# Half of the second expert table read in one pass through a token-by-expert weight matrix, with all gathers of the first table ahead of those of the second

## The reference

```python
best, pos = lax.top_k(cand, PEER_TOPK)                        # 8 heads x 16 experts per token
expert_idx = jnp.take_along_axis(cand_idx, pos, axis=-1)
gates = jax.nn.softmax(best, axis=-1).astype(h.dtype)
...
act = jnp.einsum('td,thkd->thk', xb, u_tab[ib])
w = gb * jax.nn.gelu(act, approximate=False)
return jnp.einsum('thk,thkd->td', w, v_tab[ib])
```

## Time and profile before

| what | value |
|---|---|
| time, median of 3 runs | 2583.87 us (2572.18 to 2584.49) |
| profiled execution: span from first to last instruction | 2569.2 us |
| around the span, median of the runs less the span | 14.7 us |
| PE / DVE / POOL / ScalarE busy | 76% / 50% / 32% / 10% |
| bytes moved by DMA | 793 MB, of which 606 MB by POOL's queue |

### The profile page before, as it was taken

The page is one execution under the profiler, slowest core; times in us unless marked ns, Lnnn a source line. Parts: engine busy times, 40 slices in busy tenths (PEclk is TensorE's granted clock), DMA queues, the critical chain, the costliest instruction groups (busy, mean ns, idle before and its releaser), DMA issues.

```text
span 2569.2 us, 20124 instructions
## 1 busy us (share of the span) xinstructions
PE 1958.5 (76%) x7000; PEld 1310.4 (51%) x7000; DVE 1286.4 (50%) x1645; ACT 266.1 (10%) x521; POOL 824.4 (32%) x583
## 2 busy tenths in 40 slices
PE   0399999998999999896895569557855774586557
PEld 0388888887888888785332223223322332232223
DVE  8634587773222221488644754474456324532553
ACT  0012122111000000201111001100101010001001
POOL 1000000000000000033555655565566555655652
PEclk9999999999999999998997789778877987897788
DMA  9867765662434354177999999999999999999996
GB/s 399 371 248 305 292 284 221 250 261 109 153 136 158 134 222 151 56 302 327 361 392 392 392 391 393 389 374 387 392 383 369 402 390 367 366 411 389 400 362 269
DMA packets 92366, 793.07 MB, mean 309 GB/s; under 512 B 10657, under 2 KB 10657, under 8 KB 11313
## 3 DMA queue, kind: packets, MB, share of 16 engines
q0 software_dynamic: 78512, 606.14, 59.0%
q1 hardware_dynamic: 13824, 186.55, 18.8%
q10 hardware_dynamic: 2, 0.02, 0.0%
HBM read 790.57 MB, written 2.10 MB: 309 GB/s over the span
## 4 chain that ended last, share of the span: by engine, by line
PE 57%; DMA 16%; issue 9%; DVE 8%; POOL 8%; ACT 1%; POOLq 0%; DVEq 0%; SPq 0%; ACTq 0%
PE ps L559 26%; PE ps L720 19%; DMA arena<-expert_u,u_now 11%; PE ps L567 9%; POOL arena L370 7%; DMA arena<-ada 3%; DVE arena L1018 3%; DMA arena<-expert_v,v_now 2%; DVE mod_rows L761 1%; DVE work L857 1%; DVE work L854 1%; DVE buf_b L769 1%; PE ps L575 1%; PE ps L674 0%; POOL v_now L363 0%
## 5 line engine op out<-in xcount | busy, mean ns | idle before, releaser
L720 PE MATMUL ps<-arena,work 128*128 128x512 f32 x1520 | 698.1, 619 | 446.6 <-ACT work L534 284.8
L1018 DVE CUSTOM_DVE_ANT_0 arena<-arena,buf_b 128x2048 f32<-128x2048 f32 x256 | 586.0, 2293 | 427.6 <-DMA arena<-expert_u,u_now 424.4
L720 PEld LDWEIGHTS ps<-arena,work 128*128 128x128 f32 x1520 | 301.4, 200 | 837.5 <-issue 461.0
L370 POOL DMA_INDIRECT arena<-expert_u,u_now x256 | 477.7, 1866 | 293.1 <-DVE work L1018 142.3
L559 PE MATMUL ps<-buf_a,arena 128*128 128x256 f32 x2304 | 508.1, 382 | 10.9 <-DVE arena L875 5.2
L559 PEld LDWEIGHTS ps<-buf_a,arena 128*128 128x128 f32 x2304 | 440.9, 192 | 75.0 <-issue 14.7
L370 POOL DMA_INDIRECT arena<-expert_v,v_now x192 | 231.3, 1204 | 258.9 <-PE ps L720 216.7
L559 PE MATMUL ps<-arena 128*128 128x256 f32 x1024 | 223.7, 379 | 1.0 <-ACT arena L496 1.0
L720 PE MATMUL ps<-mod_rows,work 128*128 128x512 f32 x504 | 221.5, 592 | 0.0
L559 PEld LDWEIGHTS ps<-arena 128*128 128x128 f32 x1024 | 193.9, 190 | 27.3 <-issue 1.3
L350 POOL DMA_DIRECT2D arena<-ada x32 | 16.9, 529 | 529.4 <-DVE mod_rows L761 489.3
(11 more groups left out here) (194 smaller groups left out, 1010.1 us busy)
## 6 DMA issues: line engine op xcount, KB each, us to landing
arena<-weights SPq DMA_DIRECT2D x68, 2048.0 KB, 9.2
arena<-ada POOLq DMA_DIRECT2D x32, 2048.0 KB, 12.0
arena<-ada SPq DMA_DIRECT2D x16, 2048.0 KB, 16.3
arena<-expert_u,u_now POOLq DMA_INDIRECT x256
arena<-expert_v,v_now POOLq DMA_INDIRECT x192, 10.8
buf_a<-x_t SPq DMA_DIRECT2D x1, 2048.0 KB, 20.7
arena<-ln_rows POOLq DMA_DIRECT2D x1, 2048.0 KB, 7.4
buf_a<-x_rows SPq DMA_DIRECT2D x1, 2048.0 KB, 8.2
```

What stands on the lines that cost most here:

```text
L370: pool.indirect_dma_start(slots[s], None, table, bass.IndirectOffsetOnAxis(ap=indices[:, e:e + 1], axis=0)).then_inc(ring_loaded[s], 16)
L720: last = mm(ps[:, 4 * b + n, :], diag[:, s], v_slot[s][:, n * 512:(n + 1) * 512], start=first and e == 0, stop=False, skip_group_check=True)
L1018: v.tensor_tensor_reduce(out=u_slot[s], in0=u_slot[s], in1=h2[:, b], scale=1.0, scalar=0.0, op0=ALU.mult, op1=ALU.add, accum_out=sums[:, e ...
```

## The change

- Table `v` is split on the host by columns. Columns 0 to 1023 become `v_pass`, with the rows reordered so that 128 consecutive rows are the experts that share the second of the two key numbers (expert = 128 x first + second). Columns 1024 to 2047 become `v_side`.
- `v_side` is gathered as before, but with 4 KB per token, 0.524 MB per gather, in 5 slots, alternating between the blocks. DVE adds each gathered row, times its weight, into PSUM banks 4 to 7 (`add_row`).
- `v_pass` is read whole, once: 128 loads of 128 x 1024 (0.524 MB) by SP into 4 slots. PE multiplies each with a weight matrix [128 experts, 128 tokens] for each block, 4 products of 512 columns per load, into banks 0 to 3.
- The weight matrix is made in 64 groups of 4 tokens. For one token, the 128 slots are on the partitions: `first_hot` [slot, first key] is 1 where the slot's expert has that first key, `second_hot` [slot, second key] is the weight where it has that second key, and one PE product of the two gives the token's weights for all 16,384 experts, as 128 x 128. ScalarE copies a group from PSUM into `weight_t` (`keep_group`). The expert numbers and weights are transposed by PE for this.
- Groups 0 to 31 (block 0) are made beside the `u` gathers of block 1's heads 1 to 7, with `first_hot` built by ScalarE. Groups 32 to 63 (block 1) come after the last `u` row, with both built by DVE, and after each one `add_row`.
- All 256 gathers of `u` come first, in one ring of 8 slots, straight from `expert` without copies, and then the 256 of `v_side`. Loops over heads are written out.
- SP's first four pass loads wait only for the last choice (`s_gt`). PE starts the pass once all 64 groups are kept.
- On ScalarE the exponential of late choice n (`soft_exp`) stands between the gelus of heads n - 1 and n; the diagonals (L534), the three vector rows and `merge_block0`'s place in the middle go. Both blocks are merged and normalised at the end.
- `arena` grows to 8 chunks, `buf_b` moves into it, and the constants grow by 112 columns.

```diff
-U_RING, V_RING = 4, 8
-VECTOR_ROWS = (9, 11, 13)
+U_RING = 8
+SIDE = D_MODEL // 2
+PASS_RING, GATHER_RING = 4, 5
+GROUP = 4
+GROUPS = TOKENS // GROUP
+GROUP_BANKS = 3
...
+        u_first = [arena[:, n * row:(n + 1) * row] for n in range(4)] + [shift2, scale2]
+        u_slot = [u_first + [arena[:, n * row:(n + 1) * row] for n in pair] for pair in ((14, 15), (6, 7))]
+        weight_t = [arena[:, n * 4 * CHUNK:(n + 1) * 4 * CHUNK].rearrange("p (n t) -> p n t", t=P) for n in (1, 0)]
+        rows_out = chunk(5).rearrange("p (b n) -> p b n", b=BLOCKS)
+        gather_slot = [gate1[:, 0:SIDE], shift2[:, 0:SIDE], shift2[:, SIDE:], scale2[:, 0:SIDE], scale2[:, SIDE:]]
+        keys = cst[:, C_IOTA:C_END]
+        first_hot = cst[:, C_LEVELS:C_IOTA].rearrange("p (s t n) -> p s t n", s=2, t=GROUP)
+        second_hot = gate1[:, SIDE:].rearrange("p (s t n) -> p s t n", s=2, t=GROUP)
+        tail_slots = work[:, 0:PASS_RING * SIDE]
+        pass_slot = [tail_slots[:, n * SIDE:(n + 1) * SIDE] for n in range(PASS_RING)]
+        def groups_beside(n):
+            first = (n - HEADS - 1) * 5
+            return range(first, min(first + 5, GROUPS // BLOCKS))
...
+            sp.wait_ge(s_gt, BLOCKS * HEADS)
+            for n in range(N_KEYS):
+                s = n % PASS_RING
+                if n >= PASS_RING:
+                    sp.wait_ge(pass_used[s], n // PASS_RING)
+                sp.dma_start(pass_slot[s], v_pass[n * P:(n + 1) * P, :]).then_inc(pass_loaded[s], 16)
+                if n == 32 + PASS_RING:
+                    sp.dma_start(ln_slot[1], ln_rows[2:4, :].partition_broadcast(P)).then_inc(s_ln[1], 16)
...
+            def gather(table, into, b, e, loaded_sem):
+                pool.indirect_dma_start(into, None, table, bass.IndirectOffsetOnAxis(ap=expert[:, b, e:e + 1], axis=0))\
+                    .then_inc(loaded_sem, 16)
+            for n in range(BLOCKS * HEADS):
+                wait_alone(pool, s_ex, n + 1)
+                for e in range(TOPK):
+                    r = n * TOPK + e
+                    s, turn = r % U_RING, r // U_RING
+                    if turn:
+                        wait_alone(pool, u_used[s], turn)
+                    if r == SLOTS:
+                        for q in range(2):
+                            wait_alone(pool, used[q], 1 + F_END[q])
+                    gather(expert_u, u_slot[n // HEADS][s], n // HEADS, n % HEADS * TOPK + e, u_loaded[s])
+            for r in range(BLOCKS * SLOTS):
+                s, turn = r % GATHER_RING, r // GATHER_RING
+                if turn:
+                    wait_alone(pool, gather_used[s], turn)
+                elif s:
+                    wait_alone(pool, u_used[4 + (s - 1) // 2], BLOCKS * SLOTS // U_RING)
+                gather(v_side, gather_slot[s], r % BLOCKS, r // BLOCKS, gather_loaded[s])
...
+            def gelu(n):
+                act_e.wait_ge(u_used[U_RING - 1], (n + 1) * TOPK // U_RING)
+                run(gel[n % 2], act[n % 2], ACT.Gelu).then_inc(s_gel, 1)
+            def keep_weights_t(b):
+                act_e.wait_ge(s_wtp, b + 1)
+                run(wgt_t[:, b * P:(b + 1) * P], ps[:, 3, P:2 * P], ACT.Copy).then_inc(s_wt, 1)
+            def build_first_hot(g):
+                if g >= 2:
+                    act_e.wait_ge(s_grp, g - 1)
+                slot = first_hot[:, g % 2]
+                for t in range(GROUP):
+                    me.step(run(slot[:, t], keys, ACT.Abs, bias=first_t[:, g * GROUP + t:g * GROUP + t + 1], scale=-1.0))
+                me.settle()
+                run(slot, slot, ACT.Relu, bias=1.0, scale=-1.0).then_inc(s_fh, 1)
+            def keep_group(g):
+                act_e.wait_ge(s_grp, g + 1)
+                b, t = g // (GROUPS // BLOCKS), g % (GROUPS // BLOCKS) * GROUP
+                run(weight_t[b][:, :, t:t + GROUP], ps[:, g % GROUP_BANKS, :].rearrange("p (t n) -> p n t", t=GROUP), ACT.Copy)\
+                    .then_inc(s_grpe, 1)
+            gelu(0)
+            soft_exp(HEADS + 1)
+            for n in range(1, HEADS):
+                soft_exp(HEADS + 1 + n)
+                gelu(n)
+            keep_weights_t(0)
+            gelu(HEADS)
+            act_e.wait_ge(s_idx, 1)
+            for n in range(HEADS + 1, BLOCKS * HEADS):
+                for g in groups_beside(n):
+                    build_first_hot(g)
+                    if g:
+                        keep_group(g - 1)
+                gelu(n)
+            keep_group(GROUPS // BLOCKS - 1)
+            keep_weights_t(1)
+            for g in range(GROUPS // BLOCKS, GROUPS):
+                keep_group(g)
+            for b in range(BLOCKS):
+                rstd_of_ln(b, BLOCKS + 1 + b)
...
+            def transpose_experts(b):
+                pe.wait_ge(s_exr, b + 1)
+                nc.tensor.transpose(ps[:, 3, 0:P], expert_rows, ident).then_inc(s_ext, 1)
+            def transpose_weights(b):
+                pe.wait_ge(s_wgt, (b + 1) * HEADS)
+                pe.wait_ge(s_idx, BLOCKS)
+                nc.tensor.transpose(ps[:, 3, P:2 * P], gates[:, b], ident).then_inc(s_wtp, 1)
+            def multiply_groups(groups):
+                for g in groups:
+                    pe.wait_ge(s_fh, g + 1)
+                    pe.wait_ge(s_sh, g + 1)
+                    if g >= GROUP_BANKS:
+                        pe.wait_ge(s_grpe, g - GROUP_BANKS + 1)
+                    for t in range(GROUP):
+                        last = mm(ps[:, g % GROUP_BANKS, t * P:(t + 1) * P], first_hot[:, g % 2, t], second_hot[:, g % 2, t],
+                                  start=True, stop=True)
+                    last.then_inc(s_grp, 1)
             pe.wait_ge(s_top, 1 + HEADS)
             pe.wait_ge(s_late, 1 + HEADS)
             for b in range(BLOCKS):
...
+                transpose_experts(b)
+            for b in range(BLOCKS):
+                transpose_weights(b)
+                multiply_groups(range(b * GROUPS // BLOCKS, (b + 1) * GROUPS // BLOCKS))
+            pe.wait_ge(s_grpe, GROUPS)
+            for n in range(N_KEYS):
+                s = n % PASS_RING
+                pe.wait_ge(pass_loaded[s], (n // PASS_RING + 1) * 16)
+                for b in range(BLOCKS):
+                    for c in range(2):
+                        last = mm(ps[:, 2 * b + c, :], weight_t[b][:, n], pass_slot[s][:, c * 512:(c + 1) * 512],
+                                  start=n == 0, stop=n == N_KEYS - 1)
+                    if n == N_KEYS - 1:
+                        last.then_inc(s_sum, 1)
+                if n < N_KEYS - 1:
+                    last.then_inc(pass_used[s], 1)
...
+            def reduce_rows(n, which):
                 for e in which:
...
+                    r = n * TOPK + e
+                    s = r % U_RING
+                    dve.wait_ge(u_loaded[s], (r // U_RING + 1) * 16)
+                    rows = u_slot[n // HEADS][s]
+                    v.tensor_tensor_reduce(out=rows, in0=rows, in1=h2[:, n // HEADS], scale=1.0, scalar=0.0,
+                                           op0=ALU.mult, op1=ALU.add, accum_out=act[n % 2][:, e:e + 1]).then_inc(u_used[s], 1)
+            def weigh(n):
+                dve.wait_ge(s_gel, n + 1)
+                mine = gates[:, n // HEADS, n % HEADS * TOPK:(n % HEADS + 1) * TOPK]
+                v.tensor_tensor(mine, gel[n % 2], mine, ALU.mult).then_inc(s_wgt, 1)
+            def indices_by_slot(b):
+                if b:
+                    dve.wait_ge(s_ext, b)
+                v.tensor_copy(expert_rows, expert[:, b]).then_inc(s_exr, 1)
+                dve.wait_ge(s_ext, b + 1)
+                c = slice(b * P, (b + 1) * P)
+                me.link(v.tensor_copy(index_t[:], ps[:, 3, 0:P]))
+                me.link(v.tensor_scalar(half_t[:], index_t[:], 7, None, ALU.logical_shift_right))
+                me.link(v.tensor_copy(first_t[:, c], half_t[:]))
+                me.link(v.tensor_scalar(half_t[:], index_t[:], N_KEYS - 1, None, ALU.bitwise_and))
+                v.tensor_copy(second_t[:, c], half_t[:]).then_inc(s_idx, 1)
+            def build_first_hot(g):
+                t = slice(g * GROUP, (g + 1) * GROUP)
+                v.tensor_tensor(first_hot[:, g % 2], keys.unsqueeze(1).to_broadcast([P, GROUP, N_KEYS]),
+                                first_t[:, t].unsqueeze(2).to_broadcast([P, GROUP, N_KEYS]), ALU.is_equal).then_inc(s_fh, 1)
+            def build_second_hot(g):
+                for t in range(GROUP):
+                    c = slice(g * GROUP + t, g * GROUP + t + 1)
+                    last = v.tensor_scalar(second_hot[:, g % 2, t], keys, second_t[:, c], wgt_t[:, c], ALU.is_equal, ALU.mult)
+                last.then_inc(s_sh, 1)
+            def add_row(r):
+                s, b, e = r % GATHER_RING, r % BLOCKS, r // BLOCKS
+                dve.wait_ge(gather_loaded[s], (r // GATHER_RING + 1) * 16)
+                sums = ps[:, 4 + 2 * b:6 + 2 * b, :].rearrange("p a n -> p (a n)")
+                if e == 0:
```

(93 more changed lines are left out.)

217 lines of the change are left out of this document (43 added, 174 removed).

## The result

The changed kernel takes 2,455.13 us (median of 4 runs, 2,454.11 to 2,456.62) against 2,579.01 us before (4 runs, 2,572.18 to 2,584.49): ratio on record 0.9529, 95% interval 0.9499 to 0.9559 (the two medians alone give 0.9520). The profiled execution has a span of 2,452.0 us and took 2,454.11 us in all. All four runs took 2.1 us more than their span.

What follows compares the result with a forecast made beforehand. Transfers at 388 GB/s bound the kernel, DVE close behind. Head 0's end at 1,217.8, block 0 to 1,555.5, block 1 328, then 6, groups 86, last stretch 460, end 30, plus 14.7 around the span: 2,480 us; range 2,436 to 2,560.

Steps and rivals of the forecast that it cites:

- around the span: Time outside the profiled span: 14.7 us added to the span of 2,465.5 us, holding to the median of the runs.
- Block 1: Its eight heads have DMA and DVE almost level: DMA 328 us at 400 GB/s, DVE 320 us; ends at 1,883.5.
- rival A: Faster: DMA keeps 424 GB/s whenever it is the limit, block 1 DVE-bound at 320 us; 2,436 us, chance 0.15.
- The groups: Groups 32 to 63: DVE does first_hot, second_hot and add_row, together 2.7 us each, 86 us for 32.
- Rival C: Smaller gain: the 32 groups take 4.1 us each, DVE waiting for PE and ScalarE; 2,525 us, chance 0.13.
- The last stretch: Pass and remaining gathers: 179.8 MB at 400 GB/s, 450 us, plus 10 us for gathers left over; ends at 2,435.5.
- PE 225 us: In the pass, PE's 512 products start 0.44 us apart and take 225 us, hidden behind transfers.
- PE at 1.8 us per load and waiting for loads: Sign that the forecast is right: in the pass PE takes 1.8 us per load and waits for loads.
- the clause on half clock: In the pass at half clock, PE's products would take about 450 us, still just hidden.
- The last 95 gathers alone: With equal shares the pass is through after 325 us; 95 gathers then run with five slots, 10 us added.
- rival D: Smaller gain: pass takes the larger share, 95 gathers left over run at 1.8 us; 2,527 us, chance 0.09.
- Rival B: Last stretch, slower: half-sized gathers keep a 10.8 us landing, 2.66 us per gather with five slots; 2,603 us, chance 0.07.

Runs made afterwards that it cites:

- the last experiment: The kernel before, with the exponential of the next late choice queued after 4 of a head's 16 diagonals instead of after all: 2,573.05 us, ratio 1.0001.
- the kernel with equal shares: The changed kernel without the pass's products for token block 1, except for its first and last load: 2,476.65 us.
- the first four kernels: Changed kernel with half of PE's products (2,476.65 us), half the loads (2,430.58), both (2,405.10), or four slots for second-table gathers (2,501.08).

## Why the forecast was right, and where it was not

The forecast was 2,480 us, 24.9 above the measured median. Step by step, in us of the span:

| step | forecast | measured |
|---|---|---|
| head 0 ends | 1,217.8 | 1,219.4 |
| block 0 done | 1,555.5 | 1,551.1 |
| last reduction ends | 1,883.5 | 1,872.1 |
| pass starts | 1,975.5 | 1,967.4 |
| last addition ends | 2,435.5 | 2,423.1 |
| span | 2,465.5 | 2,452.0 |
| around the span | 14.7 | 2.1 |

*Block 0* went as said: DVE-bound, heads 45.9 us apart (46.7 forecast), no wait at the exponential. The stall's going is no gain by itself, though: in the kernel before it was covered by transfers, as the last experiment shows. It counts here only because DVE now sets the pace.

*Block 1* took 321 us and not 328. The forecast had DMA setting it by a little over DVE, at 400 GB/s. Measured were 409 over the window, and DVE was busy in 317.5 of 319 us, near the 320 of the forecast's own sum for DVE. That is rival A's case for this stage.

*The groups* took 2.88 us each, not 2.7. Counted from start to start, `second_hot` took 1.02 us (0.83 forecast, bound 1.10), `add_row` 1.26 (1.22) and `first_hot` 0.60 (0.69); the mis-sized term is `second_hot`. Rival C's hand-over between engines did not come about.

*The last stretch* took 455.7 us against the 460 forecast, and the reason given for it was partly wrong. DMA at about 400 GB/s and POOL's 0.95 us per gather were right. "PE 225 us", hidden either way, was not. I took the 0.44 us between starts for one product, but an fp32 product of 128 x 512 leaves two records: 1,024 for the 512 products of the pass. One product costs 0.856 us, a load 3.43 us, the pass 438 us. So the sign "PE at 1.8 us per load and waiting for loads" failed: PE took 3.43 us per load and hardly waited. PE is nearly level with the transfers, and the clause on half clock was wrong by more. The first records of the pass ran at a granted clock of 0.50 and start 0.85 us apart:

```profile
1970.11 0.34 PEld L761 LDWEIGHTS ps<-work,arena 128*128 128x128 f32 x1 [0.52 <-issue]
1970.96 0.23 PEld L761 LDWEIGHTS ps<-work,arena 128*128 128x128 f32 x1 [0.52 <-issue]
```

At that pace (an estimate from these rows) the 1,024 records would need some 870 us and set the end of the kernel. What spared the forecast is that the granted clock was 0.99 of 2.4 GHz over the stretch, after 0.50 in the stage before. This was luck: the forecast gave no reason for a full clock, and PE's true 438 us happened to lie just under what the transfers needed. The last 95 gathers alone at 1.31 us, for which I added 10 us, don't exist, because PE holds the loads back. Where such a stretch was made, each gather took 1.6 us, between the forecast's 1.31 and rival D's 1.8.

*Rival B* (2,603 us) fell; even with one slot fewer the kernel is at 2,501 us. Two things in its paragraph don't hold. The gathers would set the stretch from 460 / 219 = 2.10 us each on; the 2.57 us named there is only where the whole gain would be gone. With five slots they came every 2.06 us, right beside that point, and with four, at 2.31, they were past it. And 10.8 us x 388 GB/s = 4.2 MB is what four gathers of 1.05 MB carry, not twelve. So that product says nothing for queueing in twelve slots. What speaks for queueing is the median landing of a 0.52 MB gather, 10.7 us in the kernel with equal shares and 5.9 us with gathers alone. The Trainium skill, "DMA: Bandwidth & Descriptors", section Bandwidth, which spoke for this rival, asks for 1 MiB per DMA to reach 75% of the peak. The trace disagrees for DMAs of half that size: 402 to 409 GB/s with nine slots. It agrees in direction with only five: 324 to 326.

*Around the span* I took 14.7 us, by setting the profiled execution at the median. The changed kernel adds 2.1 us to its span in each of its runs, and the kernel before 1.7 us (2,573.67 against a span of 2,572.0 in the run beside the first four kernels). The profiled execution of before took about 2,569.2 + 1.7 = 2,570.9 us and simply lay 13.0 us under the median of its three runs, a matter of the kernel's spread: over 15 runs it goes from 2,559.4 to 2,585.3 us. Against the profiled execution (2,454.1 us) the forecast is 26.1 us off by the table. This term carries 12.6 of it, the earlier end of block 1 11.4, the groups take 3.3 back, the last stretch gives 4.3 and the end 1.1.

*Where the 124 us come from.* The bytes alone bring nothing: with four `u` slots and 67 MB fewer the kernel takes 2,576 us. With eight slots in one stream of `u`, DVE never waits for a row from 1,118 to 1,872 us, and the last reduction ends 120 us sooner. That doesn't make the bytes worthless. As an estimate from these rows, the second table's 256 whole rows, 268 MB at the 409 GB/s of block 1, would take 656 us after 1,872, where the changed kernel needs 550 for groups, pass and gathers. So some 100 us hang on the split once the slots are there, and no run has eight slots without it. *What stays open*: why the kernel before holds 388 GB/s rather than 409 or 424 with its 12 slots. A landing of 10.8 us at 388 GB/s means that on average only some four of its rows are on their way. The stall isn't the reason, and nothing else of it was tried.

## What to carry to other kernels

Fewer bytes pay only where enough buffers keep the engine behind them fed across its longest other task: here the same change gained 124 us with eight slots over a 10.4 us choice, and nothing with four. Before calling an engine hidden, count its records per operation, not only the distance between them. And where two streams share the transfers, ask which ends first, since a faster consumer can take the share that the longer stream needs.

## What the runs showed of the hardware

- An fp32 product of 128x128 by 128x512 is two records, 0.428 us apart at a granted clock of 0.99 to 1.00 (0.856 us) and 0.85 us apart at 0.50.
- Two DMA queues with work always waiting got equal shares in the kernel with half of PE's products (a load per 2.56 us, a gather per 2.56 us, both of 0.524 MB). By the Trainium skill, "DMA: Bandwidth & Descriptors", section "Queues, rings and completion order", each DMA engine goes round-robin between its queues; the trace agrees.
- Rows of 4 KB ran at 406 to 410 GB/s in most slices of the last stretch, rows of 8 KB in the `u` stage at up to 429.
- A gather's instruction on POOL took 0.95 us on average in the stretches where DVE's instructions have a PSUM operand, and 1.95 us (192 of `u`) where they have two SBUF operands.
- Four 128-column instructions with a scalar per partition (L1085) take 1.02 us from the first start to the next instruction's, though each is recorded with a median of 0.35 us.
